# Expert routing in 16 bits, one exponential for all token blocks, and an earlier start of the expert groups in a two-layer trunk

## The chip, the cores and the metric

The kernel runs on one core of one Trainium2 chip. The metric is the time of one execution on the device in microseconds. The kernel before took 3550.75 us as the median of three runs (3548.97 to 3553.28).

## The reference

Two layers, each with a mixer (sliding-window attention beside a convolution module) and then an expert retrieval. The change lies in the retrieval alone:

```python
def peer(h, w_query, sub_keys, u_tab, v_tab):
    q = (xt @ w_query).reshape(T, N_RET_HEADS, 2, HALF_KEY)
    s = jnp.einsum('thpd,hpnd->thpn', q, sub_keys).astype(jnp.float32)
    s_half, i_half = lax.top_k(s, TOPK_HALF)                     # 16 best of 128, per head and half
    cand_s = (s_half[:, :, 0, :, None] + s_half[:, :, 1, None, :])...
    cand_i = (i_half[:, :, 0, :, None] * N_KEYS + i_half[:, :, 1, None, :])...
    top_s, pos = lax.top_k(cand_s, TOPK)                         # 16 best pairs of 256
    ids = jnp.take_along_axis(cand_i, pos, axis=-1)
    gates = jax.nn.softmax(top_s, axis=-1)
    # per token: y = sum over 8 heads x 16 experts of gate * gelu(u_id . x) * v_id
```

T is 512 tokens, there are 8 heads, 128 keys a side, 16384 experts and 1024 features.

## The kernel before

**Layout.** All activations lie transposed (features on the 128 partitions). Every weight comes as a tile of 128 x 1024 numbers of 512 KB from one long stream in HBM, in the order of its use, through four slots `raw`. ScalarE (ACT) rounds a tile to `w_hi` (L911), and VectorE (DVE) or GpSimd (POOL) writes the remainder into `w_lo`. TensorE (PE) multiplies hi by hi, hi by lo and lo by hi, so a tile costs 24 matmuls (L589 to L591, in `product`). PE waits for `lo_done` before each tile. The load of tile n + 4 into a slot waits until tile n is multiplied.

**The retrieval** has three stages in each layer:

1. *Queries and half scores*, 16 tiles. DVE finds the 16 best of each half score row (`top16`).
2. *U tiles 0 to 127*. The first 128 tokens take the sparse way: the rows of their 128 experts are gathered from HBM by POOL's indirect DMA (L539) into four slots `gbuf`, and DVE takes the dot product of each row with the token (L1610, `dot`). The other 384 tokens take the dense way: PE multiplies every U tile with them (128 x 384 outputs), ACT applies Gelu and stores the result to HBM.
3. *V tiles 0 to 127* (L847 to L849), weighed by gate times Gelu.

**Inside the U stage** the work lies like this:

- DVE first does the routing, one block of 128 tokens after the other (`for tt in range(NB)`, four blocks). For each: the candidates' sums (L1652), the indices as floats (L1658), the 16 best (L1618 to L1628), the place of each in the table of pairs (L1665 to L1682), and then the *look-up of the indices*: for each of the two sides compare a 128 x 2048 field with 0..15 (L1686), multiply with the indices (L1693) and sum over 16 (L1697), all in float32. DVE subtracts the row's maximum (L1670), ACT takes the exponential (L1162) ahead of U tiles 8, 16, 24 and 33 (`EXP_TILES`), and DVE sums it up and writes the gates (L1709 to L1714). Behind the first block's look-up stand the gather ids (L1705, L1706).
- As long as DVE routes, POOL writes the `w_lo` of the U tiles: tiles 0 to `U_ROUTE` - 1 = 39, one instruction of 128 x 1024 each (L523, `low`). At tile `GATHER_TILE` = 20 it waits for the ids and then puts the first four gathers between the lows.
- From tile 40 DVE writes `w_lo` itself (L1724, `u_low`). Ahead of that it waits until POOL's are done.
- PE transposes the routes behind tile `U_ROUTE` + 2 (L833). Then come 48 *groups* of 8 tokens: DVE builds two one-hot fields and two gated ones (L1758 to L1763, 16-bit), and PE multiplies them (L819, L821, 16 matmuls) into a map of gates over all experts. Group g stands behind tile `C_FIRST + g * C_TILES // 48` with 43 and 75, so from tile 43 to tile 116. With each group DVE also takes 2 or 3 dots (`DOTS_BY_GROUP` = 114 over 48 groups), and POOL issues the gather of a freed slot (L539) behind a small addition (L553) that waits for the dot.

The order on each engine is the order of the code: nothing is rescheduled.

Of the kernel before, what the change touches and what calls it, by code (L numbers as in the profile page):

```python
# [25 lines left out]
P = 128  # L26
# [16 lines left out]
U_ROUTE = 40  # L43
C_FIRST, C_TILES = 43, 75
# [6 lines left out]
EXP_TILES = (8, 16, 24, 33)  # L51
SLOTS = 4
GATHER_TILE = 20
# [9 lines left out]
TOP_STEPS = RH * 45 + NB * 65 + 2  # L63
# [100 lines left out]
def build_trunk(nc, stream, u_rows, ada, params_d, keys_d, con_d, x_d, c_d, pos_d, c_scr, g_scr, out_d):  # L164
    with ExitStack() as ctx:
# [99 lines left out]
        esum = at("esum", small + 6656, [P, 2, RH])  # L265
# [248 lines left out]
        def _(pool):  # L514
# [43 lines left out]
        def _(pe):  # L558
# [13 lines left out]
            with pe.Fori(0, DEPTH) as l:  # L572
# [307 lines left out]
        def _(act):  # L880
# [24 lines left out]
            with act.Fori(0, DEPTH) as l:  # L905
# [307 lines left out]
        def _(dve):  # L1213
# [85 lines left out]
            with dve.Fori(0, DEPTH) as l:  # L1299
# [347 lines left out]
                for tt in range(NB):  # L1647
                    v4 = v16[:, tt].rearrange("t (h p) k -> t h p k", p=2)
                    c0 = 0
                    for a0, a1, nb in PAIRS:  # L1650
# [14 lines left out]
                    mark(nc.vector.tensor_copy(esum[:, 0:1].rearrange("t o h -> t h o"), t16[:, :, 0:1]))  # L1665
# [4 lines left out]
                    nc.vector.tensor_tensor(t16[:], t16[:], esum[:, 0].rearrange("t (h o) -> t h o", o=1)  # L1670
                                            .broadcast_to([P, RH, TOPK]), ALU.subtract).then_inc(g_exp, 1)
# [13 lines left out]
                    for p in range(2):  # L1685
                        mark(nc.vector.tensor_tensor(  # L1686
                            eq[:], abf[:, p].rearrange("t (k o) -> t k o", o=1).broadcast_to([P, RH * TOPK, TOPK]),
                            con[:, K_IOTA:K_IOTA + TOPK].rearrange("t (o a) -> t o a", o=1)
                            .broadcast_to([P, RH * TOPK, TOPK]), ALU.is_equal))
                        settle()  # L1690
                        i4 = i16f[:].rearrange("t (h p) a -> t h p a", p=2)[:, :, p]
                        e4 = eq[:].rearrange("t (h k) a -> t h k a", h=RH)
                        mark(nc.vector.tensor_tensor(  # L1693
                            e4, e4, i4.rearrange("t h (o a) -> t h o a", o=1).broadcast_to([P, RH, TOPK, TOPK]),
                            ALU.mult))
                        settle()
                        mark(nc.vector.tensor_reduce(routed[:, tt, p], eq[:], AX, ALU.add))  # L1697
                        settle()
# [9 lines left out]
                    dve.wait_ge(g_exp, 2 * (l * NB + tt) + 2)  # L1708
                    mark(nc.vector.tensor_reduce(esum[:, 1], t16[:], AX, ALU.add))  # L1709
                    settle()  # L1710
# [6 lines left out]
                    if tt >= 1:  # L1717
                        ins.then_inc(rt_ready, 1)
# [207 lines left out]
```

## Time and profile before

| | us |
|---|---|
| median of the runs | 3550.75 |
| the profiled execution | 3548.25 |
| its span | 3546.4 |
| PE busy | 3417.1 (96%) |
| DVE busy | 3012.6 (85%) |
| ACT busy | 1575.2 (44%) |
| POOL busy | 1401.6 (40%) |

The span is the time from the first to the last instruction; 1.85 us of the execution lie around it. A busy share is an average over stages that have different limits: in the mixer the DMA engines are nearly idle, in the U and V stages they are nearly always busy. For a wait it says which engine's instruction came last. The rows of the section below are in us from the start of the span. The first layer's U stage begins at 643.4 and its V stage at 1243.8, the second layer's at 2395.3 and 2999.8.

### The profile page before, as it was taken

How to read it: one execution, taken by the hardware profiler on the slowest of the kernel's cores; microseconds unless marked ns; L12 is line 12 of the kernel's file. 1: busy time of each engine (PE TensorE's matmuls, PEld its weight loads, DVE VectorE, ACT ScalarE, POOL GpSimd, SP SyncE). 2: the span in 40 equal slices, each digit the busy share in tenths (PEclk: the TensorE clock that was granted, in tenths of full speed). 3: DMA queues.
4: the chain of work that ended last, by engine and by line, in shares of the span. 5: the costliest groups of instructions: out<-in, count | busy, mean ns of one | idle time of the engine just before them, and what ended most of it. 6: DMA issues, size and time to landing. Idle time of an engine off the chain costs nothing.

```text
span 3546.4 us, 61171 instructions
## 1 busy us (share of the span) xinstructions
PE 3417.1 (96%) x19318; PEld 3142.4 (89%) x19318; DVE 3012.6 (85%) x5973; ACT 1575.2 (44%) x2335; POOL 1401.6 (40%) x1140
## 2 busy tenths in 40 slices
PE   6999999999999999999999999999999999999999
PEld 5767778999999999999977777789999999999999
DVE  6799877998888788888868997789988897888888
ACT  3474434444555433333345734434455554333333
POOL 0000003575666555446500000137666664544543
PEclk9999999999999999999999999999999999999999
DMA  5112272468999999999921123635699999999998
GB/s 196 66 60 72 89 257 99 144 196 272 370 375 354 329 340 347 348 344 327 335 79 60 60 79 110 230 107 166 193 321 362 353 356 324 356 354 332 345 347 286
DMA packets 408601, 863.51 MB, mean 243 GB/s; under 512 B 165520, under 2 KB 231056, under 8 KB 407952
## 3 DMA queue, kind: packets, MB, share of 16 engines
q1 hardware_dynamic: 297456, 539.62, 45.3%
q0 software_dynamic: 73728, 268.47, 21.1%
q10 hardware_dynamic: 37152, 52.45, 4.0%
q8 instruction: 98, 1.61, 0.2%
q14 instruction: 167, 1.37, 0.1%
HBM read 774.41 MB, written 85.98 MB: 243 GB/s over the span
## 4 chain that ended last, share of the span: by engine, by line
issue 50%; PE 26%; POOL 18%; DMA 3%; DVE 2%; POOLq 0%; ACT 0%; SPq 0%; DVEq 0%; ACTq 0%
POOL w_lo L523 7%; PE ps L847 7%; PE ps L849 7%; PE ps L848 7%; POOL gbuf L539 6%; POOL spare L553 5%; DMA raw<-stream 2%; PE ps L589 1%; PE ps L591 1%; PE ps L590 1%; DMA gbuf<-u_rows,ids_u 0%; DMA gelu_scratch<-g_out 0%; DVE w_lo L1799 0%; POOLq L552 0%; DMA cg<-gelu_scratch 0%
## 5 line engine op out<-in xcount | busy, mean ns | idle before, releaser
L911 ACT CAST w_hi<-raw 128x1024 fp32r<-128x1024 f32 x680 | 715.8, 1055 | 886.8 <-DMA raw<-stream 850.4
L589 PE MATMUL ps<-h_hi,w_hi 128*128 128x384 f32 (+1 forms) x2944 | 1064.6, 362 | 15.4 <-DVE w_lo L1724 12.7
L591 PE MATMUL ps<-h_hi,w_lo 128*128 128x384 f32 (+1 forms) x2944 | 1036.7, 352 | 0.0
L590 PE MATMUL ps<-h_lo,w_hi 128*128 128x384 f32 (+1 forms) x2944 | 1035.9, 352 | 0.0
L847 PE MATMUL ps<-cf_hi,w_hi 128*128 128x384 f32 x2048 | 692.5, 338 | 13.3 <-DVE w_lo L1799 8.5
L848 PE MATMUL ps<-cf_lo,w_hi 128*128 128x384 f32 x2048 | 690.1, 337 | 0.0
L849 PE MATMUL ps<-cf_hi,w_lo 128*128 128x384 f32 x2048 | 689.9, 337 | 0.0
L553 POOL TENSOR_TENSOR spare<-spare 128x1 f32<-128x1 f32 x504 | 359.2, 713 | 777.7 <-DVE y_sp L1778 478.0
L589 PEld LDWEIGHTS ps<-h_hi,w_hi 128*128 128x128 f32 x2944 | 554.6, 188 | 72.2 <-DVE w_lo L1724 17.3
L590 PEld LDWEIGHTS ps<-h_lo,w_hi 128*128 128x128 f32 x2944 | 555.2, 189 | 38.6 <-issue 5.7
L591 PEld LDWEIGHTS ps<-h_hi,w_lo 128*128 128x128 f32 x2944 | 554.2, 188 | 37.3
L523 POOL TENSOR_TENSOR w_lo<-raw,w_hi 128x1024 fp32r<-128x1024 f32 x112 | 317.1, 2839 | 240.2 <-ACT w_hi L911 239.9
L847 PEld LDWEIGHTS ps<-cf_hi,w_hi 128*128 128x128 f32 x2048 | 386.5, 189 | 17.5 <-DVE w_lo L1799 14.2
L849 PEld LDWEIGHTS ps<-cf_hi,w_lo 128*128 128x128 f32 x2048 | 386.5, 189 | 0.0
L848 PEld LDWEIGHTS ps<-cf_lo,w_hi 128*128 128x128 f32 x2048 | 386.5, 189 | 0.0
L539 POOL DMA_INDIRECT gbuf<-stream,ids_v x256 | 368.3, 1439 | 37.6 <-POOL spare L553 1.7
L531 POOL TENSOR_TENSOR spare<-spare 128x1 f32<-128x1 f32 x2 | 0.4, 195 | 941.8 <-DVE w_lo L1304 941.8
L539 POOL DMA_INDIRECT gbuf<-u_rows,ids_u x256 | 354.4, 1384 | 40.1 <-POOL spare L553 5.5
L1610 DVE CUSTOM_DVE_ANT_1 gbuf<-gbuf,h_tok 128x1024 f32<-128x1024 f32 x256 | 304.7, 1219 | 45.1 <-DMA gbuf<-u_rows,ids_u 44.5
L1778 DVE SCALAR_TENSOR_TENSOR y_sp<-gbuf,a_sp,y_sp 128x1024 f32<-128x1024 f32 x256 | 327.0, 1277 | 3.6 <-DMA gbuf<-stream,ids_v 3.6
L1395 DVE SCALAR_TENSOR_TENSOR yT<-uT,lp,yT 128x512 f32<-128x512 f32 x480 | 327.5, 744 | 0.0
L1799 DVE TENSOR_TENSOR w_lo<-raw,w_hi 128x1024 fp32r<-128x1024 f32 x256 | 311.7, 1217 | 0.0
(254 smaller groups left out, 4540.6 us busy)
## 6 DMA issues: line engine op xcount, KB each, us to landing
raw<-stream SPq DMA_DIRECT2D x682, 512.0 KB, 5.2
gelu_scratch<-g_out ACTq DMA_DIRECT2D x256, 192.0 KB, 5.8
cg<-gelu_scratch SPq DMA_DIRECT2D x256, 192.0 KB, 6.0
c_scratch<-stage SPq DMA_DIRECT2D x64, 512.0 KB
cg<-c_scratch SPq DMA_DIRECT2D x256, 128.0 KB, 5.1
qT<-ada SPq DMA_DIRECT2D x32, 512.0 KB, 6.1
cgate<-ada SPq DMA_DIRECT2D x32, 512.0 KB, 5.4
w_rows<-ada SPq DMA_DIRECT2D x32, 512.0 KB, 7.4
```

What stands on the lines that cost most here:

```text
L523: nc.gpsimd.tensor_tensor(w_lo[:, s], raw[:, s], w_hi[:, s].bitcast(F32), ALU.subtract).then_inc(lo_done, 1)
L539: nc.gpsimd.indirect_dma_start(out=gbuf[:, n % SLOTS], out_offset=None, in_=table, in_offset=bass.IndirectOffsetOnAxis(ap=ids[:, k:k + 1], ...
L553: nc.gpsimd.tensor_tensor(spare[:, 16:17], spare[:, 17:18], spare[:, 18:19], ALU.add).then_inc(room, 1)
L589: nc.tensor.matmul(ps[:, b, 0:n], wh, hi[:, c, t0:T], start=c == 0, stop=False)
L590: nc.tensor.matmul(ps[:, b, 0:n], wh, lo[:, c, t0:T], start=False, stop=False)
L591: mm = nc.tensor.matmul(ps[:, b, 0:n], wl, hi[:, c, t0:T], start=False, stop=c == C - 1)
L847: nc.tensor.matmul(ps[:, c, P:T], w_hi[:, s, c], cf_hi[s][:], start=first, stop=False)
L848: nc.tensor.matmul(ps[:, c, P:T], w_hi[:, s, c], cf_lo[s][:], start=False, stop=False)
L849: mm = nc.tensor.matmul(ps[:, c, P:T], w_lo[:, s, c], cf_hi[s][:], start=False, stop=last)
L911: nc.scalar.copy(w_hi[:, s], raw[:, s]).then_inc(hi_done, 1)
L1395: ins = nc.vector.scalar_tensor_tensor(out=yT[:, c], in0=uT[:, c, k:k + T], scalar=weight, in1=yT[:, c], op0=ALU.mult, op1=ALU.add)
L1778: nc.vector.scalar_tensor_tensor(out=y_sp[:], in0=gbuf[:, k % 4], scalar=a_sp[:, bass.ds(at_k, 1)], in1=y_sp[:], op0=ALU.mult, op1=ALU.add ...
```

## The change

It has five parts.

1. **Look-up in 16 bits.** The fields are float16, and both sides are done together: the two columns of places are written twice side by side (`ab_two`), one comparison of 128 x 4096 (against `places`), one multiplication with the indices `i16h`, and in place of the sum over 16 a tree of four additions of 2048, 1024, 512 and 256 elements.
2. **One exponential.** The scores of all blocks are kept (`t16` has a block axis). Behind the last block's 16 best DVE subtracts all the maxima in one instruction, ACT takes one exponential of 128 x 512 ahead of U tile 24, and DVE writes all gates at the very end; there is one `rt_ready` for the layer.
3. **POOL's lows in four pieces** of 128 x 256 each, everywhere where POOL writes `w_lo`.
4. **Hand-over at tile 28** in place of 40 (`U_ROUTE`): POOL writes tiles 0 to 27, DVE from 28.
5. **Gathers from tile 12** in place of 20, and **groups from tile 31** over 87 tiles in place of from 43 over 75.

```diff
-U_ROUTE = 40
-C_FIRST, C_TILES = 43, 75
+U_ROUTE = 28
+C_FIRST, C_TILES = 31, 87
...
-EXP_TILES = (8, 16, 24, 33)
+EXP_TILE = 24
 SLOTS = 4
-GATHER_TILE = 20
+GATHER_TILE = 12
...
-                    nc.gpsimd.tensor_tensor(w_lo[:, s], raw[:, s], w_hi[:, s].bitcast(F32),
-                                            ALU.subtract).then_inc(lo_done, 1)
+                    for c in range(0, C, 2):
+                        part = nc.gpsimd.tensor_tensor(w_lo[:, s, c:c + 2], raw[:, s, c:c + 2],
+                                                       w_hi[:, s, c:c + 2].bitcast(F32), ALU.subtract)
+                    part.then_inc(lo_done, 1)
...
+                        pe.wait_ge(rt_ready, l + 1)
                         for tt in range(1, NB):
-                            pe.wait_ge(rt_ready, l * NBD + tt)
...
-                for tt in range(NB):
-                    while u < EXP_TILES[tt]:
-                        u_tile(u)
-                        u += 1
-                    act.wait_ge(g_exp, 2 * (l * NB + tt) + 1)
-                    nc.scalar.activation(t16[:], t16[:], ACT.Exp).then_inc(g_exp, 1)
+                while u < EXP_TILE:
+                    u_tile(u)
+                    u += 1
+                act.wait_ge(g_exp, 2 * l + 1)
+                nc.scalar.activation(t16[:], t16[:], ACT.Exp).then_inc(g_exp, 1)
...
-                    for p in range(2):
-                        mark(nc.vector.tensor_tensor(
-                            eq[:], abf[:, p].rearrange("t (k o) -> t k o", o=1).broadcast_to([P, RH * TOPK, TOPK]),
-                            con[:, K_IOTA:K_IOTA + TOPK]..., ALU.is_equal))
+                    mark(nc.vector.tensor_copy(ab_two[:], abf[:].rearrange("t p (k o) -> t p k o", o=1)
+                                               .broadcast_to([P, 2, RH * TOPK, 2])))
+                    settle()
+                    n = 2 * RH * TOPK
+                    mark(nc.vector.tensor_tensor(
+                        eq[:].rearrange("t p h k (a b) -> t (p h k) a b", b=2),
+                        ab_two[:]..., places[:]..., ALU.is_equal))
+                    settle()
+                    mark(nc.vector.tensor_tensor(e3, e3, i16h[:]..., ALU.mult))
+                    settle()
+                    for half in (8, 4, 2):
+                        mark(nc.vector.tensor_tensor(e2[:, :, 0:half], e2[:, :, 0:half], e2[:, :, half:2 * half], ALU.add))
                         settle()
-                        mark(nc.vector.tensor_reduce(routed[:, tt, p], eq[:], AX, ALU.add))
-                        settle()
+                    mark(nc.vector.tensor_tensor(routed[:, tt, 0:2]..., e2[:, :, 0:1], e2[:, :, 1:2], ALU.add))
+                    settle()
```

**DVE, the look-up of a block.** Before, behind the places of a block (`abf`), each side has its own comparison, product and sum (the rows named REGISTER_ALU hold the waits for the step before):

```order
L1682 TENSOR_TENSOR abf<-parts,line_106 128x128
L1598 REGISTER_ALU
L1686 TENSOR_TENSOR eq<-abf,con 128x2048
L1598 REGISTER_ALU
L1693 TENSOR_TENSOR eq<-eq,i16f 128x2048
L1598 REGISTER_ALU
L1697 TENSOR_REDUCE routed<-eq 128x128
L1598 REGISTER_ALU
L1686 TENSOR_TENSOR eq<-abf,con 128x2048
```

And of the change the same place, from the doubled columns on:

```order
L1694 CAST ab_two<-abf 128x512
L1601 REGISTER_ALU
L1698 TENSOR_TENSOR eq<-ab_two,places 128x4096
L1601 REGISTER_ALU
L1705 TENSOR_TENSOR eq<-eq,i16h 128x4096
L1601 REGISTER_ALU
L1711 TENSOR_TENSOR eq<-eq 128x256x8
L1601 REGISTER_ALU
L1711 TENSOR_TENSOR eq<-eq 128x256x4
L1601 REGISTER_ALU
L1711 TENSOR_TENSOR eq<-eq 128x256x2
```

Six long instructions, two of them sums, have become one cast and six that read two fields each (the sixth, the last addition into `routed`, stands behind this piece).

**POOL, where the gathers begin.** Before, at tile 20, a low is one instruction, and each of four is followed by a gather (ISA is the wait for the ids):

```order
L546 ISA
L522 REGISTER_ALU
L523 TENSOR_TENSOR w_lo<-raw,w_hi 128x1024
L539 DMA gbuf<-u_rows,ids_u 128x1024
L522 REGISTER_ALU
L523 TENSOR_TENSOR w_lo<-raw,w_hi 128x1024
```

Of the change, at tile 12:

```order
L550 ISA
L524 REGISTER_ALU
L526 TENSOR_TENSOR w_lo<-raw,w_hi 128x256 x4
L543 DMA gbuf<-u_rows,ids_u 128x1024
L524 REGISTER_ALU
L526 TENSOR_TENSOR w_lo<-raw,w_hi 128x256 x4
```

The wait stands eight tiles earlier, and every low is four instructions behind one another.

**ACT, the exponential.** Before, each of the four exponentials (here the last, ahead of tile 33) stands in front of the rounding of the tile two ahead (L911), with a table load on each side:

```order
L1161 ISA
L1162 ACT_TABLE_LOAD
L1162 ACTIVATE t_101<-t_101 128x128
L911 CAST w_hi<-raw 128x1024
L1151 REGISTER_ALU
L1152 ACT_TABLE_LOAD
```

Of the change there is one, ahead of tile 24, over all blocks:

```order
L1165 ACT_TABLE_LOAD
L1165 ACTIVATE t_103<-t_103 128x512
L915 CAST w_hi<-raw 128x1024
L1154 ISA
L1155 REGISTER_ALU
L1156 ACT_TABLE_LOAD
```

It waits for the last block, and the rounding of tile 26 stands behind it.

## Rows read from the trace of the kernel before

**Rows 1.** Windows: length, busy PE, PEld, DVE, ACT, POOL; PEclk, DMA share, GB/s.

```profile
643.40:810.60 167.20, 167.16 (x961) 166.15 (x961) 163.40 (x458) 74.55 (x94) 121.20 (x42) 1.00 0.60 181
831.10:1195.40 364.30, 354.64 (x2519) 343.84 (x2520) 328.89 (x488) 201.82 (x240) 237.16 (x224) 1.00 0.96 351
```

**Rows 2.** Waits from 643.4 to 810.6: who for whom, us in total, times, longest.

```profile
ACT t L1162 <- DVE t L1670: 3.6, 2, 2.3
PEld ps L589 <- POOL w_lo L523: 1.1, 4, 0.4
```

**Rows 3.** Waits from 810.6 to 1196, the first layer's groups.

```profile
DVE gbuf L1610 <- DMA gbuf<-u_rows,ids_u: 19.5, 15, 2.7
DVE w_lo L1724 <- ACT w_hi L911: 17.1, 16, 2.3
...
PE ps L819 <- DVE gated_lo L1763: 6.0, 7, 1.7
PE ps L589 <- DVE w_lo L1724: 5.8, 7, 1.6
```

**Rows 4.** Waits from 2562.5 to 2952, the second layer's groups.

```profile
PE ps L819 <- DVE gated_lo L1763: 7.8, 9, 1.7
PE ps L589 <- DVE w_lo L1724: 7.0, 5, 2.7
```

**Rows 5.** Timeline of PE: a group's first matmul and the next tile's.

```profile
890.06 0.23 PE L819 MATMUL ps<-gated_hi,one_i 128*128 128x128 f16 x1
...
890.97 0.42 PE L589 MATMUL ps<-h_hi,w_hi 128*128 128x384 f32 x1
```

**Rows 6.** Timeline of DVE in a group.

```profile
847.58 1.22 DVE L1724 TENSOR_TENSOR w_lo<-raw,w_hi 128x1024 fp32r<-128x1024 f32 x1
848.72 0.68 DVE L1758 TENSOR_TENSOR one_j<-numbers,ij 128x1024 f16<-128x1024 f16 x1
...
851.12 1.22 DVE L1610 CUSTOM_DVE_ANT_1 gbuf<-gbuf,h_tok 128x1024 f32<-128x1024 f32 x1
```

**Rows 7.** Timeline of DVE: start of the routing's first block, then its second block.

```profile
657.75 1.05 DVE L1652 TENSOR_TENSOR cand<-v 128x384 f32<-128x384 f32 x2
...
698.25 1.05 DVE L1652 TENSOR_TENSOR cand<-v 128x384 f32<-128x384 f32 x2
...
708.41 2.17 DVE L1665 COPY esum<-t 128x8 f32<-128x8 f32 x1
...
711.22 0.29 DVE L1672 CAST parts<-shifted 128x256 f32<-128x256 uint32 x1
...
712.78 2.29 DVE L1686 TENSOR_TENSOR eq<-abf,con 128x2048 f32<-128x2048 f32 x1
715.11 4.38 DVE L1693 TENSOR_TENSOR eq<-eq,i16f 128x2048 f32<-128x2048 f32 x1
...
731.05 0.28 DVE L1709 TENSOR_REDUCE esum<-t 128x8 f32<-128x128 f32 x1
...
731.61 2.92 DVE L1714 TENSOR_TENSOR routed<-t,esum 128x128 f32<-128x128 f32 x1
734.45 1.05 DVE L1652 TENSOR_TENSOR cand<-v 128x384 f32<-128x384 f32 x2
```

**Rows 8.** Timeline of POOL: lows, and the small addition.

```profile
699.84 2.39 POOL L523 TENSOR_TENSOR w_lo<-raw,w_hi 128x1024 fp32r<-128x1024 f32 x1 [1.66 <-ACT w_hi L911]
...
713.88 10.23 POOL L523 TENSOR_TENSOR w_lo<-raw,w_hi 128x1024 fp32r<-128x1024 f32 x3 [3.33 <-ACT w_hi L911]
...
817.75 0.21 POOL L553 TENSOR_TENSOR spare<-spare 128x1 f32<-128x1 f32 x1
```

**Rows 9.** Timeline of ACT: the third and the fourth exponential.

```profile
748.24 0.31 ACT L1162 ACTIVATE t<-t 128x128 f32<-128x128 f32 x1 [2.30 <-DVE t L1670]
...
785.47 0.31 ACT L1162 ACTIVATE t<-t 128x128 f32<-128x128 f32 x1 [1.27 <-DVE t L1670]
```

**Rows 10.** Window behind a PE wait of 2.4 us, columns as in Rows 1.

```profile
1245.00:1250.00 5.00, 5.00 (x21) 4.94 (x21) 4.09 (x9) 2.89 (x5) 1.15 (x2) 0.66 0.94 245
```

More of the change, by code:

```diff
@@ L254, in build_trunk @@
         i16 = at("i16", base + 28 * KB, [P, NB, 2 * RH, TOPK], U32)
-        eq = at("eq", base + 32 * KB, [P, RH * TOPK, TOPK])
+        eq = at("eq", base + 32 * KB, [P, 2, RH, TOPK, TOPK], F16)
         cand = at("cand", base + 40 * KB, [P, RH, CAND])
         small = base + 48 * KB
-        i16f = at("i16f", small, [P, 2 * RH, TOPK])
-        t16 = at("t16", small + 1024, [P, RH, TOPK])
+        i16h = at("i16h", small, [P, 2, RH, TOPK], F16)
+        places = at("places", small + 512, [P, TOPK], F16)
+        ab_two = at("ab_two", base + 44 * KB, [P, 2, RH * TOPK, 2], F16)
+        t16 = at("t16", base + 45 * KB, [P, NB, RH, TOPK])
         p16 = at("p16", small + 1536, [P, RH, TOPK], U32)
@@ L264, in build_trunk @@
         line4 = at("line4", small + 6144, [P, RH * TOPK])
-        esum = at("esum", small + 6656, [P, 2, RH])
+        esum = at("esum", base + 47 * KB, [P, 2, NB, RH])
         row_no = at("row_no", small + 6784, [P, 2, P])
@@ L1657, in _ @@
                         c0 += n
-                    mark(nc.vector.tensor_copy(i16f[:], i16[:, tt]))
+                    mark(nc.vector.tensor_copy(i16h[:].rearrange("t p h k -> t h p k"),
+                                               i16[:, tt].rearrange("t (h p) k -> t h p k", p=2)))
+                    mark(nc.vector.tensor_copy(places[:], iota[:, 0:TOPK]))
                     settle()
                     guard()
-                    top16([(t16[:, h], p16[:, h], cand[:, h]) for h in range(RH)])
+                    top16([(t16[:, tt, h], p16[:, h], cand[:, h]) for h in range(RH)])
                     settle()
                     pos = p16[:].rearrange("t h k -> t (h k)")
-                    mark(nc.vector.tensor_copy(esum[:, 0:1].rearrange("t o h -> t h o"), t16[:, :, 0:1]))
                     mark(nc.vector.tensor_scalar(shifted[:, 0], pos, 4, None, ALU.logical_shift_right))
@@ L1699, in _ @@
+                    mark(nc.vector.tensor_tensor(routed[:, tt, 0:2].rearrange("t p (k o) -> t (p k) o", o=1),
+                                                 e2[:, :, 0:1], e2[:, :, 1:2], ALU.add))
+                    settle()
                     if tt == 0:
@@ L1707, in _ @@
                                                 ALU.add).then_inc(ids_in, 1)
[L1708 to L1717 removed]
+                dve.wait_ge(g_exp, 2 * l + 2)
+                mark(nc.vector.tensor_reduce(esum[:, 1].rearrange("t b h -> t (b h)"), t16[:].rearrange("t b h k -> t (b h) k"),
+                                             AX, ALU.add))
+                settle()
+                mark(nc.vector.reciprocal(esum[:, 0], esum[:, 1]))
+                settle()
+                for t0, t1, gates in ((1, NB, routed[:, 1:NB, 2]), (0, 1, g_sp[:].rearrange("t (o n) -> t o n", o=1))):
+                    ins = nc.vector.tensor_tensor(gates.rearrange("t b (h k) -> t b h k", h=RH), t16[:, t0:t1],
+                                                  esum[:, 0, t0:t1].rearrange("t b (h o) -> t b h o", o=1)
+                                                  .broadcast_to([P, t1 - t0, RH, TOPK]), ALU.mult)
+                    if t0:
                         ins.then_inc(rt_ready, 1)
```

32 lines of the change are left out of this document (15 added, 17 removed).

## The prediction

> **What bounds the kernel now.** I first read the windows over the first layer's U stage. While DVE routes (tiles 0 to 39), PE is busy for 167.16 of 167.20 us, and 167.2 / 40 gives 4.18 us a tile; the DMA engines are busy for 0.60 [rows 1]. In the groups (tiles 44 to 116) PE lacks 9.7 of 364.3 us, and the DMA share is 0.96. So TensorE sets the end, and a change off PE can only gain what PE waits for, or cost what it makes PE wait for. Then the lists of waits. In the routing PE's weight loads waited for POOL's lows 4 times, 0.4 us at most [rows 2]: POOL costs nothing there, but there is no room left either. In the groups PE waited for DVE: 5.8 us for a `w_lo` and 6.0 for a gated field in the first layer [rows 3], 7.0 and 7.8 in the second [rows 4], 26.6 us in all. DVE in turn waited there for gathered rows, 19.5 us, and for `w_hi`, 17.1 us [rows 3]. That is what the change can reach: DVE is full in the groups, and the transfers that it needs are late.
>
> **The gain: the groups' pace.** PE needs 0.91 us for a group (890.06 to 890.97) [rows 5]. Before, a group comes every 75/48 = 1.56 tiles, so PE's pitch is 1.56 x 4.18 + 0.91 = 7.44 us. DVE does in it 1.56 lows of 1.14 (847.58 to 848.72), four one-hot and gated fields in 2.40 (848.72 to 851.12) and 114/48 = 2.38 dots of 1.22 [rows 6]: 1.78 + 2.40 + 2.90 = 7.08. With its wait for rows, 19.5 / 48 = 0.41, that is 7.49, all of the pitch. After, the pitch is 87/48 = 1.81 tiles, 1.81 x 4.18 + 0.91 = 8.49 us, and DVE does 2.07 + 2.40 + 2.90 = 7.37, with the same wait 7.78, 92%. The transfers relax too: 351 GB/s over 364.3 us [rows 1] are 127.9 MB; 12 more tiles bring 0.70 MB each (load and Gelu store) and 12 x 4.18 us, so 136.3 MB over (364.3 - 12 + 50) = 402 us, 339 GB/s. The waits should mostly go. What stays are those in front of the first groups, where PE waits for DVE's reading of the transposed routes; I give them 4 us for both layers, and 2.6 for stray ones. The gain is 26.6 - 6.6 = 20 us. Its bounds are 4 (the late transfers are what counts, and they are hardly less late) and 26.6 (all waits gone).
>
> **DVE's routing, free of waits.** The second block runs from 698.25 to 734.45, 36.2 us. In it four instructions have stood behind POOL: 2.17 where such a copy needs 0.17, 4.38 where its like needs 2.29 (and once more), 2.92 for 0.29: 2.0 + 2.1 + 2.1 + 2.6 = 8.8 us [rows 7]. Free of that a block is 27.4. The old look-up, 712.78 to 731.05, is 18.3, less 4.2 of such waits 14.1. The new one, by the 16-bit row of 1024 elements in 0.68 [rows 6] against 1.22 for 1024 in 32 bits, that is 0.15 fixed and 0.52 for each 1024: comparison and product 2.28 each, additions 1.2, 0.68, 0.42 and 0.42, the cast 0.6, and 0.03 between each: 8.1. The old maximum, subtraction, sums and gates, about 1.1, leave the block. So a new block is 27.4 - 14.1 + 8.1 - 1.1 + 0.1 (`places`) = 20.4.
>
> **DVE's waits for POOL, and POOL's for DVE.** They take turns: three lows together took 10.23 us in place of 7.2 [rows 8], and DVE's comparison stood 2.1 us behind one of 2.39. A piece of a quarter costs between 0.60 (nothing fixed) and 0.75 (0.2 fixed, as the small addition of 0.21 [rows 8] has it). For DVE that is good, a wait of 0.6 in place of 2.1, but there are about 15 instructions in a block that can meet one; if all did, 9 us, if none, 0. I take 5 a block, since POOL works for 4 x 0.68 of each 4.18 us and the six of the look-up follow each other closely. For POOL it is bad: a low whose four pieces fall behind comparison, product, first and second addition takes 2.1 + 2.1 + 1.1 + 0.5 + 4 x 0.65 = 8.4 us. A low starts 6.1 us ahead of its tile (699.84 for tile 15, which PE begins at 643.4 + 15 x 4.18 = 706.1) [rows 8], so such a low makes PE wait 2.3, and one that meets less nothing. One low in each block is in that place: 4 x (0 to 2.3), I take 4 us a layer. No room hides this [rows 2].
>
> **The one exponential.** Before, the third exponential began at 748.24, ahead of tile 24, and PE's tile 26 was on the edge [rows 9, 2]. The new one stands at the same tile with POOL's low longer by 0.0 to 0.6, so its due time is about 747.6. It needs the fourth block's scores, which before came at 785.4 [rows 9], 37.8 us too late. By the new block: the routing begins at 657.8 [rows 7]; three blocks are 61.2, the gather ids add 0.9, and the fourth block's head up to the subtraction is 711.22 - 698.25 - 2.0 + 0.5 = 11.5. That makes 731.4 free of waits, and with 5 us of waits for each of 3.4 blocks 748.4: on the edge, late by 1 us. The three exponentials that go cost nothing before (ACT is busy for 74.55 of 167.2 us [rows 1]) and bring nothing.
>
> **The hand-over at tile 28.** Behind the subtraction DVE has 1.6 (711.22 to 712.78), the look-up 8.1, sum and gates 1.6 and 4 to 5 us of waits: 764.2. PE wants tile 28 at 643.4 + 28 x 4.18 = 760.4, by then 5 us later because of the waits above, so 765.4; a low by DVE is 1.2. Late by nothing to 1, I take 1. The gather ids come at 657.8 + 20.4 + 0.9 + 5 = 684, and POOL reaches tile 12 at 699.84 - 3 x 4.18 = 687.3: no wait. The four gathers there leave POOL little to catch up for three tiles; they are in the 4 us.
>
> **Sum.** Cost 4 + 1 + 1 = 6 a layer, 12 in all; its bounds are 0 and, with every low at its worst (9.2), the exponential 6 us late and 2 at the hand-over, 17 a layer. A PE wait of 2.4 us at 1241 also brought the clock to 0.66 in the next 5 us, 1.2 GHz for part of it, where 21 matmuls ran in place of 29 [rows 10]: 1.4 to 1.9 us more for each long wait; at the bound two of them a layer, so 21 a layer, 42 in all. I take none. 3548.25 - 20 + 12 = 3540.25 for the profiled execution, which lies 2.5 under the median of the runs; for the median 3542.8, and I say 3542.
>
> **The rivals.**
>
> *The routing costs nothing.* DVE and POOL meet less than I take, every block ends by 24 us, the exponential is early (744) and no PE wait arises. For it: some 9 us of each block, the search for the 16 best, read one field only. Against it: the edge in [rows 2]. Then 3548.25 - 22 + 2.5 = 3529.
>
> *The exponential decides, and the kernel is slower.* Place: ACT ahead of tile 24, with the rounding of tile 26 behind it. Point: the last subtraction later than 747.6, so waits above 4.8 us a block. At 7 us a block it ends at 755, PE waits 7.5 at tile 26, the clock falls behind it (1.9), and lows at 2.0 each in four blocks make the rest: 17 + 4 a layer, 42 in all. 3548.25 + 42 - 20 + 2.5 = 3573. For it: all of PE's margin is used up before, and 16 instructions a block can meet 4 pieces each low. Against it: pieces free DVE sooner. What the Trainium skill states speaks for it: by "SBUF — State Buffer", section "Who interferes with whom", whichever of the two comes first keeps the shared pair for its whole instruction and the other is fully blocked, so four pieces can be blocked four times; by that rule a low costs up to the 8.4 above, and the trace agrees as far as it goes (10.23 for three lows).
>
> *The transfers keep the groups' waits.* A gather's landing, not DVE's load, makes the waits of [rows 3]; 339 GB/s is still near the 351. Gain 4, cost 12 or less: 3553 to 3559.
>
> *The 16-bit look-up isn't double rate.* Then comparison, product and tree take 13.9 in place of 8.1, each block 5.8 more, the exponential 20 us late in each layer: 3590 to 3600. Against it: the 16-bit fields of the groups, also with a repeated pair innermost, take 0.68 for 1024 [rows 6]. The Trainium skill ("VectorE: DVE Perf Modes", section "What auto-detection actually checks") wants every tensor in 16 bits with step 1 for the double rate; by that rule the last addition alone, which writes 32 bits, runs at the single one, and at 256 elements that is 0.42 as taken above.
>
> **How the numbers follow.** Forecast 0.40, with its own range of 3534 to 3551; nothing for the routing 0.25 (3529); the exponential 0.17 (3573); the transfers 0.13; single rate 0.05. What a measurement of this kernel can tell is about 0.2%, 7.1 us, so faster means under 3543.6 and slower over 3557.9. Forecast: 0.22 faster, 0.18 same. Routing free: 0.25 faster. Exponential: 0.04 same, 0.13 slower. Transfers: 0.08 same, 0.05 slower. Single rate: 0.05 slower. Faster 0.47, same 0.30, slower 0.23. The range reaches from 3526 (all 26.6 gained, nothing lost) to 3567, part of the way to the exponential's case.
>
> **What would show it.** In the groups: PE's waits for `w_lo` and the gated fields at about 3 us a layer in place of 11.8 and 14.8, DMA at 340 GB/s. In the routing: lows of 3 us alone and of 6 to 8.5 during the look-up, DVE blocks of 25 us, waits of PE for POOL of 1 to 2 us about once a block, the one exponential at about 748. The forecast is wrong if PE waits over 5 us at tile 26 or 28, if there are no waits for POOL at all, or if the groups still wait over 8 us a layer.

## The result and the profile after

The changed kernel takes 3563.38 us (median of 16 runs) where the kernel before takes 3551.61 (16 runs beside them). The ratio is 1.0026, with a 95% interval from 1.0014 to 1.0038: slower by 0.26%, about 9 us, where 3542 was forecast. The profiled execution took 3568.66 us, its span is 3566.8 (before 3546.4). The table gives the stages in us. Each runs from its first matmul to that of the next stage, the last one to its own last matmul; the second profile is that of "The change a second time" below.

| Stage | before | after | after, second profile |
|---|---|---|---|
| U, layer 1 | 600.4 | 609.3 | 613.0 |
| V, layer 1 | 542.5 | 540.1 | 542.8 |
| mixer, layer 2 | 609.0 | 611.0 | 610.7 |
| U, layer 2 | 604.5 | 608.2 | 607.4 |
| V, layer 2 | 540.4 | 548.1 | 536.5 |

The two U stages are 12.6 us longer in the first profile and 15.5 in the second, so the loss lies there. The 7.7 us by which the second V stage is longer do not come again. These are windows of the changed kernel's first layer (length, busy PE, PEld, DVE, ACT, POOL; PEclk, DMA share, GB/s): the routing, the groups, and the five microseconds behind two long waits of PE.

```profile
642.80:767.40 124.60, 113.15 (x632) 111.55 (x632) 121.35 (x447) 46.43 (x59) 103.54 (x106) 0.97 0.57 168
794.60:1202.00 407.40, 402.89 (x2809) 394.09 (x2809) 343.13 (x500) 221.64 (x264) 225.15 (x224) 1.00 0.95 336
714.00:719.00 5.00, 5.00 (x21) 5.00 (x21) 4.92 (x14) 0.00 (x0) 5.00 (x7) 0.66 0.24 91
765.30:770.30 5.00, 4.96 (x19) 4.96 (x20) 4.83 (x8) 0.00 (x0) 4.02 (x4) 0.62 0.00 0
```

Against [rows 1] both halves have changed, in opposite ways. In the groups PE lacks 4.5 of 407.4 us where it lacked 9.7 of 364.3, and the transfers run at 336 GB/s, not 351. In the routing PE now lacks 11.5 of 124.6 us; before it lacked nothing. The waits in the groups follow, three rows of the first layer and two of the second: who waited for whom, us in total, how often, the longest.

```profile
DVE gbuf L1613 <- DMA gbuf<-u_rows,ids_u: 6.3, 9, 1.9
DVE w_lo L1742 <- ACT w_hi L915: 64.0, 36, 3.6
PE ps L823 <- DVE gated_lo L1781: 5.9, 8, 1.4
...
PE ps L823 <- DVE gated_lo L1781: 5.4, 8, 1.4
PE ps L593 <- DVE w_lo L1742: 1.1, 2, 0.7
```

DVE waits 6.3 us for gathered rows, not 19.5 [rows 3], and 64.0 for `w_hi`, not 17.1: it has time left. PE's waits for a gated field and for `w_lo` are 5.9 in the first layer (before 11.8 [rows 3]) and 6.5 in the second (before 14.8 [rows 4]). That is the gain. This is the price, every wait of PE for POOL's lows in the timeline of PE, the two layers one behind the other (start, us; in brackets the wait before it):

```profile
682.22 0.44 PE L593 MATMUL ps<-h_hi,w_hi 128*128 128x384 f32 x1 [1.72 <-POOL w_lo L526]
713.76 0.44 PE L593 MATMUL ps<-h_hi,w_hi 128*128 128x384 f32 x1 [2.15 <-POOL w_lo L526]
737.28 0.44 PE L593 MATMUL ps<-h_hi,w_hi 128*128 128x384 f32 x1 [0.88 <-POOL w_lo L526]
742.51 0.44 PE L593 MATMUL ps<-h_hi,w_hi 128*128 128x384 f32 x1 [0.79 <-POOL w_lo L526]
765.34 0.69 PE L593 MATMUL ps<-h_hi,w_hi 128*128 128x384 f32 x1 [5.91 <-POOL w_lo L526]
2442.56 0.44 PE L593 MATMUL ps<-h_hi,w_hi 128*128 128x384 f32 x1 [1.72 <-POOL w_lo L526]
2474.76 0.44 PE L593 MATMUL ps<-h_hi,w_hi 128*128 128x384 f32 x1 [2.78 <-POOL w_lo L526]
2499.17 0.44 PE L593 MATMUL ps<-h_hi,w_hi 128*128 128x384 f32 x1 [1.73 <-POOL w_lo L526]
2524.30 0.69 PE L593 MATMUL ps<-h_hi,w_hi 128*128 128x384 f32 x1 [3.85 <-POOL w_lo L526]
```

They come once or twice in each block of DVE's routing, and the last of each layer, at tile 26, is the largest. The clock adds to them: in the five microseconds behind 2.15 us and behind 5.91 us it was granted at 0.66 and 0.62, that is at 1.2 GHz for part of them, and 21 and 19 matmuls lie there where 29 would at the full clock. With the clock's part (each gap together with the slow matmuls behind it, against 0.172 us for a matmul) PE loses 16.1 us in the first routing and 15.5 in the second.

Now what DVE and POOL did meanwhile. The timeline of DVE, in the look-up of the second block and around the subtraction of the fourth:

```profile
704.17 2.71 DVE L1698 TENSOR_TENSOR eq<-ab_two,places 128x4096 f16<-128x4096 f16 x1
706.92 2.29 DVE L1705 TENSOR_TENSOR eq<-eq,i16h 128x4096 f16<-128x4096 f16 x1
709.25 3.87 DVE L1711 TENSOR_TENSOR eq<-eq 128x2048 f16<-128x2048 f16 x3
713.15 1.07 DVE L1713 TENSOR_TENSOR routed<-eq 128x256 f32<-128x256 f16 x1
...
754.97 0.69 DVE L1678 TENSOR_TENSOR t<-t,esum 128x512 f32<-128x512 f32 x1
...
757.60 2.71 DVE L1698 TENSOR_TENSOR eq<-ab_two,places 128x4096 f16<-128x4096 f16 x1
760.35 2.70 DVE L1705 TENSOR_TENSOR eq<-eq,i16h 128x4096 f16<-128x4096 f16 x1
763.08 3.85 DVE L1711 TENSOR_TENSOR eq<-eq 128x2048 f16<-128x2048 f16 x3
```

The timeline of POOL in the first layer, and in the second the low of tile 26 alone; four pieces are one tile's:

```profile
665.92 2.82 POOL L526 TENSOR_TENSOR w_lo<-raw,w_hi 128x256 fp32r<-128x256 f32 x4 [1.35 <-ACT w_hi L915]
...
707.73 12.66 POOL L526 TENSOR_TENSOR w_lo<-raw,w_hi 128x256 fp32r<-128x256 f32 x12
...
757.34 11.97 POOL L526 TENSOR_TENSOR w_lo<-raw,w_hi 128x256 fp32r<-128x256 f32 x8 [5.49 <-ACT w_hi L915]
...
2516.29 7.96 POOL L526 TENSOR_TENSOR w_lo<-raw,w_hi 128x256 fp32r<-128x256 f32 x4 [3.44 <-ACT w_hi L915]
```

And the timeline of ACT at the one exponential, in the first layer and in the second:

```profile
755.69 0.63 ACT L1165 ACTIVATE t<-t 128x512 f32<-128x512 f32 x1 [2.38 <-DVE t L1678]
756.23 1.03 ACT L915 CAST w_hi<-raw 128x1024 fp32r<-128x1024 f32 x1
...
2514.64 0.64 ACT L1165 ACTIVATE t<-t 128x512 f32<-128x512 f32 x1 [0.31 <-DVE t L1678]
```

A low alone takes 2.82 us, where it took 2.39 in one piece [rows 8]. The low of tile 26 takes 7.9 us in both layers. It starts just ahead of the fourth block's comparison, and its four pieces take 0.82, 2.77, 2.77 and 1.70 us: behind each piece DVE has one instruction, and POOL stands until that is through. The Trainium skill ("SBUF — State Buffer", section "Who interferes with whom") states that whichever of the two comes first holds the ports they share for its whole instruction, and the other is blocked. The trace agrees: DVE's comparison and product stand 0.42 us behind a piece (2.71 for 2.29), and the pieces of 2.77 us have stood through them.

PE wanted tile 26 at 759.43 in the first layer, 2.2 us after its `w_hi`, and at 2520.45 in the second, 4.2 us after it. So a low of 2.82 us would have made it wait 0.7 us in the first layer and nothing in the second, where the exponential had hardly been waited for (0.31 us). The rest of the 5.91 us, and all of the 3.85, comes from the pieces' meeting the look-up.

### The profile page after: what moved, and what is told of

Its sections match the earlier page's. It is cut to its first block, busy times and chain, and to the rows that moved or that the text cites. A ratio compares the mean times of both kernels' runs of the same rounds, so it can differ in the third digit from the quotient of the medians.

```text
span 3566.8 us, 61363 instructions
## 1 busy us (share of the span) xinstructions
PE 3424.7 (96%) x19318; PEld 3149.7 (88%) x19318; DVE 2957.2 (83%) x5985; ACT 1560.4 (44%) x2317; POOL 1379.4 (39%) x1380
## 4 chain that ended last, share of the span: by engine, by line
issue 42%; PE 34%; POOL 13%; DMA 6%; DVE 3%; ACT 1%; POOLq 0%; SPq 0%; DVEq 0%; ACTq 0%
POOL w_lo L526 8%; PE ps L851 7%; PE ps L852 7%; PE ps L853 7%; PE ps L593 5%; DMA raw<-stream 5%; PE ps L595 4%; PE ps L594 4%; POOL gbuf L543 3%; POOL spare L557 2%; DMA cg<-gelu_scratch 1%; DVE gbuf L1613 1%; PE ps L823 1%; PE ps L825 1%; DVE w_lo L1817 1%
## 5 line engine op out<-in xcount | busy, mean ns | idle before, releaser
L593 PE MATMUL ps<-h_hi,w_hi 128*128 128x384 f32 (+1 forms) x2944 | 1066.5, 362 | 25.1 <-POOL w_lo L526 21.5
L557 POOL TENSOR_TENSOR spare<-spare 128x1 f32<-128x1 f32 x504 | 342.9, 680 | 875.4 <-DVE y_sp L1796 475.0
L526 POOL TENSOR_TENSOR w_lo<-raw,w_hi 128x256 fp32r<-128x256 f32 x352 | 305.5, 901 | 181.5 <-ACT w_hi L915 181.1
L1742 DVE TENSOR_TENSOR w_lo<-raw,w_hi 128x1024 fp32r<-128x1024 f32 x200 | 243.6, 1221 | 153.9 <-ACT w_hi L915 153.4
L543 POOL DMA_INDIRECT gbuf<-u_rows,ids_u x256 | 353.1, 1379 | 39.9 <-POOL spare L557 9.1
L535 POOL TENSOR_TENSOR spare<-spare 128x1 f32<-128x1 f32 x2 | 0.4, 194 | 942.0 <-DVE w_lo L1307 942.0
```

Source lines behind the costliest of these rows:

```text
L526: part = nc.gpsimd.tensor_tensor(w_lo[:, s, c:c + 2], raw[:, s, c:c + 2], w_hi[:, s, c:c + 2].bitcast(F32), ALU.subtract)
L543: nc.gpsimd.indirect_dma_start(out=gbuf[:, n % SLOTS], out_offset=None, in_=table, in_offset=bass.IndirectOffsetOnAxis(ap=ids[:, k:k + 1], ...
L557: nc.gpsimd.tensor_tensor(spare[:, 16:17], spare[:, 17:18], spare[:, 18:19], ALU.add).then_inc(room, 1)
L593: nc.tensor.matmul(ps[:, b, 0:n], wh, hi[:, c, t0:T], start=c == 0, stop=False)
```

## The experiments

Each was timed beside runs of the kernel before, and a ratio is to those runs. Their median was 3552.48 us for the first four experiments, 3549.58 for the next four and 3555.02 for the last four, so between these sets the ratios are the better measure. Waits of PE are over the whole run where no window is named, and U gives the two layers' U stages.

**One piece.** In the changed kernel:

```diff
-for c in range(0, C, 2):
-    part = nc.gpsimd.tensor_tensor(w_lo[:, s, c:c + 2], ...)
-part.then_inc(lo_done, 1)
+nc.gpsimd.tensor_tensor(w_lo[:, s], raw[:, s], ...).then_inc(lo_done, 1)
```

> The change with POOL's lows in one piece again, nothing else. Theory A (POOL and DVE take turns at their shared reads, instruction by instruction; quarters make a low that meets the look-up long, but whole lows make DVE wait 2.1 us instead of 0.4 to 0.6): PE's short waits at tiles 9, 16 and 21 vanish, lows take 2.4 alone and at most 4.7, but the routing's blocks become longer (about 31 us instead of 28), the exponential comes at about 764 instead of 755.7, PE waits about 15 us at tile 26 and 3 to 5 us at tile 28. PE's waits from 643 to 805 grow from 16 us to about 20 a layer: slower than the change by 5 to 15 us. Rival B (the pieces alone are what costs; DVE's routing has room): PE's waits for POOL in the routing fall under 3 us a layer, and the kernel is 25 us faster than the change.

3567.41 us, ratio 1.0042 [1.0032, 1.0052]. The waits of PE for lows, and the first layer's exponential in the timeline of ACT:

```profile
PE ps L591 <- POOL w_lo L525: 32.6, 2, 16.3
```

```profile
764.72 0.63 ACT L1163 ACTIVATE t<-t 128x512 f32<-128x512 f32 x1 [18.31 <-DVE t L1676]
```

All small waits for POOL are gone and two of 16.3 us have come, one a layer, since DVE's first two blocks take 32.4 and 37.6 us with lows in one piece and the exponential comes 9 us later than in the change. Theory A has the mechanism, but not its price: 5 to 15 us over the change were expected, and 4.0 came (the ratios are 0.16% apart, and their intervals overlap). So in the change's order lows in one piece are no cure: the pieces bring the exponential forward, and that isn't enough.

**Four tiles later.** The change with everything behind the routing four tiles later:

```diff
-U_ROUTE = 28
-C_FIRST, C_TILES = 31, 87
+U_ROUTE = 32
+C_FIRST, C_TILES = 35, 83
-EXP_TILE = 24
+EXP_TILE = 28
```

> The change with the exponential ahead of tile 28 instead of 24, the hand-over at tile 32 instead of 28, groups from 35 over 83 tiles instead of from 31 over 87; quarters kept. Theory A: the long wait at tile 26 (5.9 and 3.9 us, 7.9 and 6.9 with the slow clock behind it) goes, the waits for single lows in each block (2.0, 4.0 with clock, 1 and 1) stay at 8 to 12 us a layer, with one of about 2 near tile 28 where the fourth block's look-up is. 6 to 14 us faster than the change over both layers. Rival C (the exponential's position is all of it): routing waits under 3 us a layer.

3553.64 us, 0.9997 [0.9981, 1.0013]. The waits of PE:

```profile
PE ps L593 <- POOL w_lo L526: 13.7, 8, 2.2
...
PE ps L823 <- DVE gated_lo L1781: 8.7, 12, 1.7
PE ps L593 <- DVE w_lo L1742: 7.7, 5, 3.4
```

ACT no longer waits at the exponential (768.54 and 2524.22), and the large waits at tile 26 are gone. Waits of 1.0 to 2.2 us stay, eight of them, 7.1 us in the first layer and 6.6 in the second, a little under theory A's 8 to 12. It is about 10 us faster than the change, as theory A has it, and rival C falls. In each layer the last wait, 2.23 us, is that of a low which meets the fourth block's look-up with its usual room: in the first it starts at 760.14, 6.2 us before PE wants the tile, and takes 8.4. So there are two terms: the pieces by themselves, and a low behind the exponential that meets the look-up without that room.

**The look-up alone.** 16-bit look-up and one exponential, with the places of the kernel before and lows in one piece: `U_ROUTE = 40`, `C_FIRST, C_TILES = 43, 75`, `EXP_TILE = 33`, `GATHER_TILE = 20`.

> The kernel before with the 16-bit look-up and the one exponential (ahead of tile 33) alone: hand-over at 40, gathers from 20, groups from 43 over 75 tiles, lows in one piece. Theory A: no PE waits for POOL over 0.5 us; routing ends near 795 instead of 810; in the groups PE waits as before, 12 and 15 us. Time as before within 0.2%. Rival D (the 16-bit fields themselves disturb, by a look-up that reads two fields all the time): PE waits for POOL of several us remain here too, and it is slower than before by 0.2% or more.

3547.89 us, 0.9986 [0.9973, 0.9999], as theory A has it. PE never waits for POOL. The exponential comes at 783.53, DVE's routing ends near 801 (795 was expected), and what stays is in the groups:

```profile
PE ps L821 <- DVE gated_lo L1779: 14.7, 18, 2.9
PE ps L591 <- DVE w_lo L1740: 11.0, 10, 2.5
```

That is 25.7 us, where it was 26.6 before: the look-up by itself costs nothing and hardly gains, since its time isn't used.

**The middle.** As the look-up alone, with hand-over at tile 36, `C_FIRST, C_TILES = 39, 79`, `EXP_TILE = 32`.

> One-piece lows, exponential ahead of tile 32, hand-over at 36, gathers from 20, groups from 39 over 79 tiles. Theory A: routing ends near 792 to 796, PE wants tile 36 at 794, so waits of 0 to 2 us a layer there and none for POOL; a group comes every 1.65 tiles instead of 1.56, so the groups' waits are between those of before (12 and 15 us) and of the change (7 and 9): 9 to 12 a layer. 3540 to 3548, up to 0.25% faster than before. Rival D: waits for POOL of several us a layer, not faster than before.

3550.15 us, 0.9990 [0.9977, 1.0004], over the 3540 to 3548 expected and not told apart from the kernel before. PE doesn't wait for POOL; it waits 14.7 us for gated fields and 11.5 for lows by DVE, of which 1.95 and 1.52 are at the hand-over of the two layers. With lows in one piece the blocks of DVE's routing start at 658.33, 695.07, 728.64 and 762.85. The groups' other waits fall by 3.0 us against the look-up alone (22.7 for 25.7), and the two at the hand-over, 3.5 us, take that back.

**Half the dots.** The look-up-alone version, in which a dot product reads only half of the columns (half of that product is left out):

```diff
-nc.vector.tensor_tensor_reduce(out=row, in0=row, in1=h_tok[:, :, 0:P], ...)
+nc.vector.tensor_tensor_reduce(out=row[:, 0:4], in0=row[:, 0:4], in1=h_tok[:, 0:4, 0:P], ...)
```

> The look-up-only kernel (e3) with each of DVE's dots over half of the row's columns: the second half of each expert's dot product is left out, the gathers bring the whole row as before. A dot becomes about 0.69 us instead of 1.22, so DVE has 1.3 us less of 7.1 in a group, and the DMA engines have the same to move. Theory P (DVE's load against the pitch makes the groups' waits, so that any pause for a transfer falls on PE): PE's waits of e3 in the groups (14 and 11 us) fall under 5 us a layer, most of it in front of the first two groups (1.4 and 0.5). Rival Q (late transfers make them): they stay over 10 us a layer.

3521.89 us, 0.9917 [0.9901, 0.9934]. The waits of PE, and of DVE in the window 831 to 1200:

```profile
PE ps L821 <- DVE gated_lo L1779: 4.6, 6, 1.4
PE ps L591 <- DVE w_lo L1740: 2.5, 6, 0.8
...
DVE gbuf L1611 <- DMA gbuf<-u_rows,ids_u: 41.1, 24, 4.1
```

PE's waits in the groups fall from 25.7 to 7.1 us although DVE now waits twice as long for its rows (41.1 us, where the look-up alone has 20.7 in the same window). So DVE's load, not the landing of the gathers alone, makes the groups' waits at this pace. Theory P is borne out.

**Gelu stored twice.** The look-up-alone version with a second store of each Gelu result, into a part of the scratch that nobody reads:

```diff
 act.dma_start(g_scr[u], g_out[:, b]).then_inc(g_st[b], 16)
+act.dma_start(g_scr[NKEYS + u], g_out[:, b]).then_inc(g_st[b], 16)
```

> The look-up-only kernel (e3) with each Gelu result stored a second time to HBM, 192 KB more for each U tile, about 300 KB more to the 2.8 MB of a group's pitch; DVE has nothing more to do. Theory P: the groups' waits grow only as far as rows and tiles land later, by under 10 us a layer. Rival Q: DMA is at its limit already (0.96), a pitch takes 10% more, 0.7 us for each of 48 groups: 30 us a layer more.

3594.68 us, 1.0127 [1.011, 1.0144]; U 627.7 and 627.9 us, against 603.3 and 597.8.

```profile
PE ps L821 <- DVE gated_lo L1780: 32.4, 33, 2.6
PE ps L591 <- DVE w_lo L1741: 22.3, 15, 3.5
```

192 KB more for each tile, and PE's waits double. The U stages grow by 24.4 and 30.1 us, near rival Q's 30 a layer, and theory P's "under 10 us" falls. The DMA engines were at a share of 0.99 with 370 GB/s from 850 to 1210 (the look-up alone: 0.96 and 350), and ACT waited 74.0 us for its stores (waits from 831 to 1200). So the transfers have no room for this load. Half the dots shows DVE's part and this run shows that the transfers are the next bound: neither theory alone holds. What the run doesn't part is full DMA engines and an ACT that comes late with `w_hi` because it waits for its stores.

**A faster pace.** The look-up-alone version with `C_FIRST, C_TILES = 51, 67`.

> The look-up-only kernel (e3) with the groups from tile 51 over 67 tiles instead of from 43 over 75: 1.40 tiles a group. PE's pitch is 1.40 x 4.18 + 0.91 = 6.76 us, DVE needs 1.40 x 1.14 + 2.40 + 2.90 = 6.90 and its waits. Theory P: each group is late by 0.15 us and the waits on top, so PE's waits in the groups are 25 us or more a layer, where e3 has 14 and 11; the U stage is 10 to 15 us longer in each layer, 20 to 30 us slower in all. Rival Q': the pace is not what counts: waits as in e3.

3583.05 us, 1.0098 [1.0076, 1.012], 35 us over the look-up alone by the medians and 40 by the ratios. Theory P is borne out in the waits (25 us or more a layer), and its 20 to 30 us was too little.

```profile
PE ps L821 <- DVE gated_lo L1779: 42.1, 23, 3.8
PE ps L591 <- DVE w_lo L1740: 8.6, 10, 3.0
```

With the other runs this gives the price of the pace. PE's waits for the two, less those at the hand-over: 50.7 us for groups in 67 tiles, 25.7 in 75, 22.7 in 79 and 12.4 in 87 (the change). Between 75 and 87 a tile more is worth 1.1 us of waits over both layers.

**The middle in quarters.** The middle version with lows in four pieces.

> e4 (exponential ahead of tile 32, hand-over 36, groups from 39 over 79, gathers from 20) with POOL's lows in quarters instead of one piece, nothing else. Theory A: four lows a layer meet the look-up, PE waits for POOL about 2, 2 to 3, 1 to 2 and 2 us, 8 to 10 us a layer, and nothing at the hand-over: 12 to 18 us slower than e4. Rival B': quarters cost nothing once the exponential has room: no waits for POOL, as fast as e4 or faster.

3563.77 us, 1.0046 [1.0029, 1.0063], against 0.9990 for the same kernel in one piece.

```profile
PE ps L823 <- DVE gated_lo L1781: 14.8, 22, 1.4
PE ps L593 <- POOL w_lo L526: 13.8, 8, 2.3
```

There are eight waits of 1.4 to 2.3 us, 6.7 and 7.1 us a layer where 8 to 10 were expected, though the exponential isn't late. That is 13.6 us more than in one piece by the medians (12 to 18 were expected) and 0.56%, or 20 us, by the ratios.

**Quarters alone.** The kernel before, with lows in four pieces and nothing else.

> The kernel before with one edit: POOL's low parts of w in four pieces. Theory A (a split low part costs POOL itself 0.4 us more when alone, 2.82 against 2.39, and 6 to 8 us each beside DVE's look-up, so that POOL falls behind its tiles and PE waits): PE waits for POOL's w_lo come up, three to five a layer of 1 to 3 us, 4 to 10 us a layer with what the clock loses, and the kernel is 0.1 to 0.5% slower than before: 3555 to 3568. Rival B (the split is harmless with the 32-bit look-up and only the moved exponential makes it late): no PE wait for POOL over 0.5 us, ratio 0.999 to 1.001. Rival C (the split shortens DVE's blocks of 32-bit comparisons, since DVE gets the port more often): blocks more than 3 us shorter, groups' waits as before, and ratio under 1.000. On the second layer's V stage: if the split alone makes DVE's low parts late there, PE's waits for them are 9.5 us or more; if it is something of the change's groups, 8.5 or less.

3580.66 us, 1.007 [1.0051, 1.0088]; U 617.9 and 619.0. The profiled execution, 3594.54 us, is the slowest of the six.

```profile
PE ps L591 <- POOL w_lo L524: 19.2, 8, 2.9
```

```profile
723.35 2.12 DVE L1654 TENSOR_TENSOR cand<-v 128x384 f32<-128x384 f32 x2
...
755.67 2.14 DVE L1654 TENSOR_TENSOR cand<-v 128x384 f32<-128x384 f32 x2
```

The waits of theory A are there, 9.5 us in the first layer and 9.7 in the second, and 15.3 and 15.8 with the clock's part. Its price was too small: 0.1 to 0.5% was expected, 0.7% came. Rival C's first half is right as well: DVE's third block takes 32.3 us (723.35 to 755.67), and took 39.9 before (734.45 [rows 7] to 774.38), as the two engines take turns more often. But that is worth nothing here, since the next stage waits for a tile number and PE pays. In the second layer's V stage PE waited 8.6 us for DVE's lows, between the 8.5 and the 9.5 of the expectation, which decides nothing.

**The change a second time.**

> The changed kernel a second time, nothing edited. Theory A (the waits for POOL's low parts are set by the order of the instructions): the same nine waits, each within 0.4 us of the first profile, 20 to 22.5 us in all with the longest at tile 26 at 5.5 to 6.2 us; ratio 1.0015 to 1.004. Rival B (they depend on how the first profile happened to fall): the sum differs by more than 3 us. The second layer's V stage: with theory A again 9.5 to 11 us of waits for DVE's low parts; if that was chance, 4 to 8.

3562.04 us, 1.0019 [1.0006, 1.0031].

```profile
PE ps L593 <- POOL w_lo L526: 25.1, 8, 8.0
...
PE ps L851 <- DVE w_lo L1817: 6.2, 2, 5.5
```

```profile
756.99 0.63 ACT L1165 ACTIVATE t<-t 128x512 f32<-128x512 f32 x1 [3.51 <-DVE t L1678]
...
2522.10 0.64 ACT L1165 ACTIVATE t<-t 128x512 f32<-128x512 f32 x1 [4.47 <-DVE t L1678]
```

The pattern repeats and the sizes don't quite. Small waits of 1.3 to 2.5 us stand in the same blocks, ACT waits 3.5 and 4.5 us at the exponential (2.4 and 0.3 in the first profile), and tile 26 then waits 7.04 and 7.98 us. The sum of 25.1 is 3.6 over the first profile's 21.5, more than theory A allows, and the later exponential makes the difference. The second V stage's waits for DVE's lows (8.4 us in the first profile) are not a trait of the change: here they are 0.7, and 5.5 in the first V stage.

**The first routes one tile earlier.** In the middle version, and in the look-up-alone version:

```diff
-if u == U_ROUTE + 2:
+if u == U_ROUTE + 1:
     pe.wait_ge(rt_ready, l + 1)
```

> The one-piece version with the exponential behind tile 32, hand-over at tile 36 and groups from 39, in which PE's transposes of the first routes stand behind tile 37 instead of 38. Theory A (the first groups' routes reach PE one tile late): in each layer the two waits behind the hand-over, 1.95 and 1.52 us in the one-piece run before it, fall under 0.5 us in sum, and the time falls by 2 to 5 us against that run, to 3545 to 3548, 0.9980 to 0.9990 of the kernel before. Rival B (the first routes are late for another reason, so PE now stands at the transposes themselves): the wait moves to the transposes with the same 2 to 3 us a layer, and the time stays within 1 us of 3550.

> The version with hand-over at tile 40, gathers from 20, groups from 43 and 75, one piece, in which PE's transposes of the first routes stand one tile earlier (behind tile 41). Theory A: as with the other kernel of this call, up to 2 us a layer less than the 3547.9 us of the same version without the move, so 3543 to 3547, ratio 0.9972 to 0.9986. Rival B: no change, ratio 0.9984 to 0.9988.

3544.16 us, 0.9972 [0.9958, 0.9986], and 3541.47 us, 0.9968 [0.9957, 0.9979]: both are faster than both kernels. In the middle version, PE before, at the transposes of the routes (L835) and at the first group (L821):

```profile
808.97 1.14 PE L835 MATMUL ps<-con,routed 128*128 128x128 f32 x9
...
815.67 0.23 PE L821 MATMUL ps<-gated_hi,one_i 128*128 128x128 f16 x1 [1.39 <-DVE gated_lo L1779]
```

and one tile earlier:

```profile
804.44 1.15 PE L835 MATMUL ps<-con,routed 128*128 128x128 f32 x9
...
813.75 0.23 PE L821 MATMUL ps<-gated_hi,one_i 128*128 128x128 f16 x1
```

The wait of 1.39 us, and the 0.52 at the group behind it, are gone in both layers. (The first expectation gives the sizes of the waits at the hand-over, 1.95 and 1.52; this pair was meant. At the hand-over itself 1.76 and 1.78 us stay.) The U stages are 602.2 and 597.4 us against 603.7 and 598.7, a gain of 2.8 us in all. In the look-up-alone version their sum falls by 2.2, but as 7.9 us less in the first layer and 5.7 more in the second, which the move doesn't account for. The ratios with and without the move lie 0.18% apart in both versions, more than the traces explain, and their intervals overlap.

## Why the prediction was wrong, step by step

**What failed in short.** The change was forecast 9 us faster and came 9 us slower. The gain came for the most part. The cost of the routing was taken at 6 us a layer (4 for lows in pieces, 1 for the exponential, 1 for the hand-over, none for the clock) and measured 16. The failed step is the meeting of POOL's pieces with DVE's look-up: it was priced only for lows that have 6.1 us of room, and not for the low of tile 26, behind the exponential; and the slow clock behind the waits was left out.

**The bound was read rightly.** TensorE sets the end, and only its waits moved the time. "No room" for POOL's lows behind [rows 2] was the right warning.

**The gain: 20 us forecast, 14 measured.** The groups' waits went from 26.6 to 12.4 us, a gain of 14.2, or 16 with the one slow stretch of the clock that the groups had before. The transfers came as worked out, 336 GB/s for 339, and the first groups cost 3.8 us for 4. The stray waits were taken at 2.6 and measured 8.6. The rival that the transfers keep the waits fell (half the dots). The 16-bit look-up does run at the double rate: 2.29 us for 4096 elements, where 2048 in 32 bits take the same [rows 7].

**The lows in four pieces: the failed step.** The prediction says "I take 4 us a layer" and "I take none" for the clock. In the change the small waits are 5.5 and 6.2 us a layer, and tile 26 adds 5.9 and 3.9, where 1 was taken. The mechanism was described rightly, and so was the price of a low with its usual room: a bound of 2.3 us, and 2.2 in "four tiles later". But the paragraph on the exponential gives the low behind it only "0.0 to 0.6" more. By the paragraph on the hand-over the look-up begins 1.6 us behind the subtraction, so just this low had to meet it, at up to 8.4 us, and with no room to hide that. It took 7.9. In quarters alone the small waits are 9.5 and 9.7 us, all four near the bound, so half of the bound was too little there too; the pieces meet DVE again and again until the look-up is through, as in 12.66 us for three lows.

**The clock.** The prediction had measured the slow clock behind a wait [rows 10] and left it out of the sum. Of PE's 21 waits for POOL of 2.1 us or more, in all runs, 17 brought it within the next five microseconds; in the change that was 1.8 to 3 us more for each. In the change there are two such waits a layer, and the clock and the restarts make 4.6 us of the first layer's 16.1 and 5.4 of the second's 15.5. The stated bound had two slow stretches a layer.

**The one exponential.** Forecast 748.4, measured 755.69 (756.99 in the second profile). The blocks take 29.1, 27.6 and 27.6 us (starts 657.56, 686.65, 714.26, 741.90) where 20.4 and 5 of waits were taken. The 20.4 was right: with each instruction at the shortest it has in any run, the three blocks are 21.1 (the gather ids are in it), 20.5 and 20.2 us. The waits for POOL are the rest, 8.0, 7.1 and 7.4 us, since 13 to 16 instructions of a block stand, most of them 0.4 to 0.6 us: the last addition takes 1.07 and 0.62 at its shortest, the cast of the key numbers 0.83 and 0.28, `places` 0.70 and 0.16. The term that was mis-sized is the 5 us a block, a middle between none and 9. The rival "the exponential decides" had 7 us a block, 755 and 7.5 us at tile 26, and 755.7 with 5.91, or 757.0 with 7.04, is what came. But its reason for the wait is only in part the one found. PE itself wanted tile 26 at 759.43, 7.3 us after the 752.1 of an undisturbed pace (643.4 + 26 x 4.18), so the exponential was late for it by 0.7 us in the first layer and not at all in the second. That this is near the forecast's "late by 1" is luck: both times were off by 7.3 us. Moving the exponential by four tiles removes the large wait.

**The hand-over.** Forecast 1 us, measured nothing. DVE's routing ends at 769.9, later than the 764.2 forecast, but PE had been held up by more.

**The sum.** Forecast -20 + 12. Measured, with the clock: -16 in the groups and +31.6 in the routing, together +15.6; the U stages grew by 12.6, and the 3 us between stay open. Of the 16 a layer the large wait at tile 26 is 7.9 in the first layer and 6.9 in the second; the rest is that of the small waits. Of the prediction's own signs of being wrong, "over 5 us at tile 26" is what the first layer shows. Also open is why a V stage differs by up to 12 us between two profiles of the same kernel.

## What to carry to other kernels

An engine with no slack isn't helped by cutting its instruction into pieces so that its rival waits less. The pieces meet the rival's instructions one by one, and the low that took 2.4 us takes 5 to 8. Price that worst meeting once for each period of the rival, and ask of each such instruction how much room it has there: the same low cost PE 2.2 us where it had its usual room and 5.9 where it stood behind the exponential. Add the slow clock behind waits of this size. And look first where freed time can be spent: here a faster look-up was worth only what the next hand-over could make of it, and moving the one point where PE takes over the first routes gained at least as much in the medians, though the traces explain only 2 to 3 us of that.

## What the runs showed of the hardware

- A subtraction of POOL over 1024 columns takes 2.39 us in one piece [rows 8] and 2.82 in four, 0.70 from piece to piece, so some 0.14 us are fixed in each.
- Where POOL's subtractions and DVE's two-field instructions meet, the turns change after each instruction. In the look-up pieces that need 0.7 us take 2.77 next to DVE instructions of 2.3 us and 1.1 to 1.7 next to the shorter ones, and the DVE instructions stand about 0.4 us each.
- In the change PE's waits of 0.8 to 1.7 us left the clock at 1.00 in the next five microseconds; those of 2.15 and 5.91 us brought 0.66 and 0.62. The length of one wait doesn't settle it: in "four tiles later" 2.11 us left it at 1.00, in "the look-up alone" 2.90 us left it there too, and 1.77 us brought 0.66.
- From 850 to 1210 the kernel with doubled stores moved 370 GB/s at a DMA share of 0.99.
